# Expert blocks of 127 tokens in place of 128 in the f32r products of a mixture-of-experts stage

## What is computed

```python
def swiglu(h, w_gu, w_down):
    g, u = jnp.split(h @ w_gu, 2, axis=-1)
    return (jax.nn.silu(g) * u) @ w_down

def moe_swiglu(h, w_router, w_gu, w_down):          # 512 tokens, 8 experts, TOP_K = 2
    logits = (xt @ w_router).astype(F32)
    top_logit, top_e = lax.top_k(logits, TOP_K)
    gates = jax.nn.softmax(top_logit, axis=-1)
    ...                                             # sort the 1024 assignments by expert
    y = swiglu(x_of_expert, w_gu[e], w_down[e])     # 1024 -> 2 x 3584 -> 1024
    ...                                             # out[token] += gate * y
```

## Time and profile before

| | us |
|---|---|
| median of 3 runs | 2503.71 |
| lowest and highest run | 2499.23 and 2504.51 |
| profiled execution, its own time | 2502.86 |
| its span, first to last instruction | 2501.2 |
| outside the span | 1.7 |
| expert stage, first to last f32r product of the units | 1273.2 to 2405.6 |

### The profile page before, as it was taken

How to read it: one execution, slowest core, us unless ns; L and a number is a source line. 1 busy time by engine, 2 the same in 40 slices (tenths; PEclk the granted TensorE clock), 3 DMA queues, 4 the chain that set the end, 5 groups by cost and what they waited for, 6 DMA issues and landing times.

```text
span 2501.2 us, 35301 instructions
## 1 busy us (share of the span) xinstructions
PE 2373.3 (95%) x14626; PEld 1811.2 (72%) x14626; DVE 1599.1 (64%) x1807; ACT 1213.6 (49%) x1252; POOL 204.4 (8%) x214
## 2 busy tenths in 40 slices
PE   7999998999999999769979999999999999999977
PEld 4555555588888886768767788777887778777856
DVE  7997776323232334694366688667876688667864
ACT  3645343221222223654245577556765577556753
POOL 4007533000000000000000000001000000000010
PEclk9999998999999999889979999999999999999988
DMA  7668220433332232534177799779987799778960
GB/s 196 195 207 243 84 68 26 148 105 100 101 101 93 101 101 90 175 128 160 43 253 272 280 383 376 276 271 322 394 318 277 270 382 391 257 274 310 394 241 34
DMA packets 259806, 527.94 MB, mean 211 GB/s; under 512 B 19526, under 2 KB 61098, under 8 KB 256986
## 3 DMA queue, kind: packets, MB, share of 16 engines
q1 hardware_dynamic: 230250, 481.30, 54.4%
q0 software_dynamic: 6208, 25.78, 3.4%
q10 hardware_dynamic: 23184, 18.55, 2.3%
HBM read 496.03 MB, written 45.81 MB: 217 GB/s over the span
## 4 chain that ended last, share of the span: by engine, by line
PE 79%; DVE 11%; DMA 3%; ACT 3%; issue 2%; POOL 2%; ACTq 0%; POOLq 0%; DVEq 0%; SPq 0%
PE psum L1898 36%; PE psum L1424 17%; PE psum L1723 6%; PE psum L1961 4%; PE psum L1273 2%; PE psum L1994 2%; PE psum L1299 2%; PE psum L2053 2%; PE psum L1496 1%; PE psum L1938 1%; DVE stages L840 1%; DVE stages L850 1%; DVE stages L845 1%; DVE stages L841 1%; POOL stages L1091 1%
## 5 line engine op out<-in xcount | busy, mean ns | idle before, releaser
L1898 PE MATMUL psum<-stages_r 128*128 128x512 f32 x4032 | 951.7, 394 | 1.2 <-DVE stages_r L3500 0.6
L3500 DVE TENSOR_TENSOR stages_r<-kept,stages_r 128x2048 fp32r<-128x2048 f32 x336 | 769.6, 2291 | 270.3 <-ACT stages_r L2514 269.8
L1898 PEld LDWEIGHTS psum<-stages_r 128*128 128x128 f32 x4032 | 749.3, 188 | 173.8 <-issue 18.1
L2514 ACT ACTIVATE stages_r<-kept 128x2048 fp32r<-128x2048 f32 x336 | 643.7, 1916 | 374.5 <-PE psum L1898 319.5
L1424 PE MATMUL psum<-stages_r 128*128 128x512 f32 x1920 | 437.5, 390 | 3.2 <-ACT stages_r L2080 2.7
L1424 PEld LDWEIGHTS psum<-stages_r 128*128 128x128 f32 x1920 | 360.0, 188 | 79.4 <-ACT stages_r L2080 3.1
L3153 DVE TENSOR_TENSOR stages_r<-kept,stages_r 128x2048 fp32r<-128x2048 f32 x54 | 123.8, 2292 | 338.6 <-ACT stages_r L2372 338.6
L2372 ACT ACTIVATE stages_r<-kept 128x2048 fp32r<-128x2048 f32 x54 | 103.5, 1917 | 325.8 <-PE psum L1424 219.1
L1723 PE MATMUL psum<-stages_r,stages_front_r 128*128 128x512 f32 x672 | 152.6, 389 | 0.8 <-issue 0.8
L1723 PEld LDWEIGHTS psum<-stages_r,stages_front_r 128*128 128x128 f32 x672 | 126.1, 188 | 27.3 <-issue 1.2
L1299 PE MATMUL psum<-stages,kept 128*128 128x512 f32 x256 | 115.5, 598 | 0.0
(11 more groups left out here) (445 smaller groups left out, 2346.8 us busy)
## 6 DMA issues: line engine op xcount, KB each, us to landing
kept<-in_moe_w_gu_dram SPq DMA_DIRECT2D x224, 1024.0 KB, 7.9
kept<-in_moe_w_down_dram SPq DMA_DIRECT2D x112, 1024.0 KB, 8.4
kept<-in_ffn_w_gu_dram SPq DMA_DIRECT2D x28, 1024.0 KB, 5.1
kept<-in_ev_w_in_dram SPq DMA_DIRECT2D x16, 1024.0 KB, 8.0
kept<-in_ffn_w_down_dram SPq DMA_DIRECT2D x14, 1024.0 KB, 5.1
s_output_maps<-s_output_maps_by_state SPq DMA_DIRECT2D x32, 256.0 KB, 4.8
kept<-s_input_maps SPq DMA_DIRECT2D x8, 1024.0 KB, 4.9
kept<-s_output_maps SPq DMA_DIRECT2D x8, 1024.0 KB, 6.7
```

The source lines that it names most:

```text
L1898: m = pe.matmul(out_, a, b, start=start and n == 0, stop=stop and n == len(pairs) - 1, skip_group_check=True)
L2514: act.activation(w_high[n % WSLOTS], unit_tile(n), ACT.Copy).then_inc(s_wh, 1)
L3500: dve.tensor_tensor(w_low[n % WSLOTS], unit_tile(n), w_high[n % WSLOTS], ALU.subtract).then_inc(s_ws, 1)
```

## The change

A constant CAP = P - 1 = 127 is introduced, and it takes the place of P wherever the number of tokens of a block is meant and not the 128 partitions: in the stationary operands of the units' f32r products, in the instructions that make these operands and take the results out, in the store of a block and in the plan's limits. The table y_rows keeps 128 rows for each block, so row 127 of a block is no longer stored; a further fill DMA writes these eight rows (those of the blocks of the eight experts) once before the stage. The narrow leftover products and the products of all other stages stay as they are.

```diff
+        CAP = P - 1
...
-        FILLED = 16 * len(range(NE * P, (EXTRA0 + MAXX) * P, T))
+        FILLED = 16 * (1 + len(range(NE * P, (EXTRA0 + MAXX) * P, T)))
...
+            pool.dma_start(y_rows[0:NE * P, :].rearrange("(b p) n -> b p n", p=P)[:, CAP:P, :],
+                           x[0, 0:NE * (P - CAP), :].rearrange("(b p) n -> b p n", p=P - CAP)).then_inc(s_mys, 16)
...
-                pool.dma_start(y_rows[rank * P:(rank + 1) * P, :], yblk[:, 0, :]).then_inc(s_mys, 16)
+                pool.dma_start(y_rows[rank * P:rank * P + CAP, :], yblk[0:CAP, 0, :]).then_inc(s_mys, 16)
...
-                        m = pe.transpose(psum[:, turn_bank(s_), q * P:(q + 1) * P], shid[s_ % 2][:, q * P:(q + 1) * P], ident)
+                        m = pe.transpose(psum[:, turn_bank(s_), q * P:q * P + CAP], shid[s_ % 2][0:CAP, q * P:(q + 1) * P], ident[0:CAP, 0:CAP])
...
-                            m = products(psum[:, bank, :], ((x_[:, kx, 0:P], wh[:, k, :]), (x_[:, kx, P:2 * P], wh[:, k, :]),
-                                                            (x_[:, kx, 0:P], wl[:, k, :])), kx == 0, kx == 7)
+                            m = products(psum[0:CAP, bank, :], ((x_[:, kx, 0:CAP], wh[:, k, :]), (x_[:, kx, P:P + CAP], wh[:, k, :]),
+                                                               (x_[:, kx, 0:CAP], wl[:, k, :])), kx == 0, kx == 7)
...
-                                m = products(psum[:, 4 + hf, :], ((hd[:, f, 0:P], wh[:, k, at]), (hd[:, f, P:2 * P], wh[:, k, at]),
-                                                                  (hd[:, f, 0:P], wl[:, k, at])),
+                                m = products(psum[0:CAP, 4 + hf, :], ((hd[:, f, 0:CAP], wh[:, k, at]), (hd[:, f, P:P + CAP], wh[:, k, at]),
+                                                                     (hd[:, f, 0:CAP], wl[:, k, at])),
...
-            chain.link(dve.tensor_scalar(nxt, beyond, float(P), None, ALU.is_gt))
+            chain.link(dve.tensor_scalar(nxt, beyond, float(CAP), None, ALU.is_gt))
...
-            chain.link(dve.tensor_scalar(rest, rk, float(P), -float(P), ALU.is_ge, ALU.mult))
-            chain.link(dve.tensor_scalar(past, rk, float(P), None, ALU.is_ge))
+            chain.link(dve.tensor_scalar(rest, rk, float(CAP), -float(CAP), ALU.is_ge, ALU.mult))
+            chain.link(dve.tensor_scalar(past, rk, float(CAP), None, ALU.is_ge))
...
```

More of the change, by code:

```diff
@@ L1214, in _ @@
                         hold(1).then_inc(s_ix, 1)
-                        pool.dma_start(y_rows[bass.ds((u + EXTRA0) * P, P), :], yblk[:, 0, :]).then_inc(s_mys, 16)
+                        pool.dma_start(y_rows[bass.ds((u + EXTRA0) * P, CAP), :], yblk[0:CAP, 0, :]).then_inc(s_mys, 16)
             pool.wait_ge(s_mys, extra_pool * 16 + (FILLED + 16 * STORES[NE - 1]))
@@ L2542, in hidden_high @@
                     act.wait_ge(s_ht, hidden_base(i) + (s_ + 1))
-                    act.activation(hid_s[s_ % 2][:, :, 0:P], psum[:, 6 if wide else 6 + s_ % 2, :].rearrange("p (q t) -> p q t", q=4),
-                                   ACT.Copy).then_inc(s_hdA, 1)
+                    act.activation(hid_s[s_ % 2][:, :, 0:CAP],
+                                   psum[:, 6 if wide else 6 + s_ % 2, :].rearrange("p (q t) -> p q t", q=4)[:, :, 0:CAP], ACT.Copy).then_inc(s_hdA, 1)
                 def leftover_silu(s_):
@@ L2554, in unit_act @@
                     used(i, sgate_at(s_, 1))
-                    act.activation(ssil[s_ % 2], psum[:, s_ % 2, :], ACT.Silu).then_inc(s_sil, 1)
+                    act.activation(ssil[s_ % 2][0:CAP], psum[0:CAP, s_ % 2, :], ACT.Silu).then_inc(s_sil, 1)
                     if wide:
@@ L2576, in unit_act @@
                 y_rows_free(i)
-                act.activation(yblk[:, 0, 0:512], psum[:, 4, :], ACT.Copy).then_inc(s_myA, 1)
+                act.activation(yblk[0:CAP, 0, 0:512], psum[0:CAP, 4, :], ACT.Copy).then_inc(s_myA, 1)
             act.wait_ge(s_lg, TC)
@@ L3433, in _ @@
             for m_ in (2, 3):
-                chain.link(dve.scalar_tensor_tensor(out=nxt, in0=beyond, scalar=float(m_ * P), in1=nxt, op0=ALU.is_gt, op1=ALU.add))
+                chain.link(dve.scalar_tensor_tensor(out=nxt, in0=beyond, scalar=float(m_ * CAP), in1=nxt, op0=ALU.is_gt, op1=ALU.add))
                 chain.settle()
@@ L3448, in _ @@
             chain.link(dve.scalar_tensor_tensor(out=extra, in0=over, scalar=0.0, in1=past, op0=ALU.is_ge, op1=ALU.mult))
-            chain.link(dve.tensor_scalar(rk, over, float(P), None, ALU.is_ge))
+            chain.link(dve.tensor_scalar(rk, over, float(CAP), None, ALU.is_ge))
             chain.settle()
-            chain.link(dve.scalar_tensor_tensor(out=rk, in0=over, scalar=float(2 * P), in1=rk, op0=ALU.is_ge, op1=ALU.add))
+            chain.link(dve.scalar_tensor_tensor(out=rk, in0=over, scalar=float(2 * CAP), in1=rk, op0=ALU.is_ge, op1=ALU.add))
             chain.settle()
             chain.link(dve.tensor_tensor(past, rk, toks_(key), ALU.add))
-            chain.link(dve.scalar_tensor_tensor(out=over, in0=rk, scalar=float(P), in1=toks_(big), op0=ALU.mult, op1=ALU.add))
+            chain.link(dve.scalar_tensor_tensor(out=over, in0=rk, scalar=float(CAP), in1=toks_(big), op0=ALU.mult, op1=ALU.add))
             chain.settle()
@@ L3525, in hidden_low @@
                     dve.wait_ge(s_hdA, hidden_base(i) + (s_ + 1))
-                    dve.tensor_tensor(hid_s[s_ % 2][:, :, P:2 * P],
-                                      psum[:, 6 if wide else 6 + s_ % 2, :].rearrange("p (q t) -> p q t", q=4),
-                                      hid_s[s_ % 2][:, :, 0:P], ALU.subtract).then_inc(s_hdr, 1)
+                    dve.tensor_tensor(hid_s[s_ % 2][:, :, P:P + CAP],
+                                      psum[:, 6 if wide else 6 + s_ % 2, :].rearrange("p (q t) -> p q t", q=4)[:, :, 0:CAP],
+                                      hid_s[s_ % 2][:, :, 0:CAP], ALU.subtract).then_inc(s_hdr, 1)
                     if wide:
@@ L3551, in unit_dve @@
                     dve.wait_ge(s_sil, hidden_base(i) + (s_ + 1))
-                    dve.tensor_tensor(shid[s_ % 2], ssil[s_ % 2], psum[:, 2 if wide else 2 + s_ % 2, :], ALU.mult).then_inc(s_hid, 1)
+                    dve.tensor_tensor(shid[s_ % 2][0:CAP], ssil[s_ % 2][0:CAP], psum[0:CAP, 2 if wide else 2 + s_ % 2, :], ALU.mult).then_inc(s_hid, 1)
                     split(i, sup_at(s_, 1) + WSLOTS)
@@ L3567, in unit_dve @@
                 y_rows_free(i)
-                m = dve.tensor_copy(yblk[:, 0, 512:1024], psum[:, 5, :])
+                m = dve.tensor_copy(yblk[0:CAP, 0, 512:1024], psum[0:CAP, 5, :])
                 if wide:
```

## The result

The changed kernel takes 2520.18 us (median of 4 runs, 2518.74 to 2522.82) against 2502.30 us for the kernel before (median of 4 runs, 2499.23 to 2504.51): a ratio of 1.0077, 95% interval 1.0061 to 1.0093. The forecast was 2465 us. The profiled execution took 2522.82 us, its span is 2521.2 us.

The account below looks back on a forecast made before the run. PE's rate was taken to bound the kernel; removing the f32r surplus would save 22 us in wide and 16 us in small units, -38 us from 2502.86 to 2465 us, with a range of 2457 to 2572.

Parts of the forecast that it names:

- What bounds the kernel: PE, busy 95% of the span, sets the stage; changes in the distance between products come through one to one.
- The distances: Start-to-start times of PE products: f32r 226.9 ns, fp32 429.2 (512 moving columns) and 215.9 (256); f32r pays 11.0 ns extra.
- The step that failed: Units' f32r products: a four-column-at-a-time load stops the moving side, gone at 127; 11.0 ns each, 44.4 us over 4032.
- The bounds of that step: Gain on the units' 4032 products: between 0, if the surplus is a fixed cost, and 44.4 us.
- The sum's range: Whole-kernel time of 2458 to 2481 us around 2465, with the bounds of small units and surplus.
- rival 3: Units' product loads no longer hide beneath the products: 92 ns each, +371 us, 2874 us; chance 0.04.
- something else of either sign: Whole kernel: a partial gain or another new wait, without a size; chance 0.06.
- Rival 1: Units' products: surplus belongs to f32r itself or a load going by columns; nothing changes, 2503 us; chance 0.30.
- Rival 2: Block store's 127 rows land on one DMA engine: +88 us, 2591, or 2569 with wide-unit gain; chance 0.15.
- The Trainium skill's rule on fast loads: PE weight loads: fast, in four 32-column chunks, at 128 weights and non-FP32; by its letter 127 loses it.
- Plan, fill, transposes, elementwise work at nothing: Parts beside the products: plan and elementwise 0, fill at most 0.6 us, transposes at most 0.3 us.
- The small units' DMA limit: Small units: DMA needs 116.4 us, level with PE's 116.5 after the gain; 1.5 us a unit lost waiting for tiles.

Follow-up runs that it names:

- e8: Kernel before with each f32r product of the units cut in two, 256 of the 512 moving columns each; 2547.07 us against 2502.99.
- e7: Kernel before with the units' f32r products taking 96 of 128 stationary columns, from column 0; 2507.93 us against 2502.99.
- e13: Whole changed kernel with the operands of the units' products one column later, columns 1 to 127; ratio 0.9996 to the kernel before, 2498.23 us.
- e9: Kernel before with the units' f32r products taking 127 stationary columns, columns 1 to 127; 2499.20 us against 2495.64.
- e4: Kernel before with the units' f32r products taking 124 stationary columns, from column 0; 2501.28 us against 2499.89.
- e3: Kernel before with the units' f32r products taking 126 stationary columns, from column 0; 2518.38 us against 2499.89.
- e5: Kernel before with the units' f32r products taking 125 stationary columns, from column 0; 2517.77 us against 2502.99.
- e14: Kernel before, all 128 columns, with the turned-token buffers (stationary side of gate and up products) moved by 4 bytes; 2512.03 us against 2498.83.
- e18: Kernel before, all 128 columns, with the turned-token buffers (stationary side of gate and up products) moved by 16 bytes; 2507.32 us against 2501.22.
- e2: Changed kernel with products, hidden-value transposes and elementwise work beside them back at 128; plan, fill, store and copies stay at 127; ratio 0.9998 to before.
- e17: Kernel before with the units' f32r products taking 126 stationary columns, columns 2 to 127; 2498.06 us against 2501.22.

## Why the prediction was wrong, point by point

- *What bounds the kernel.* Right. PE is on the path through all units, and a change of a product's distance came through one to one: 5 to 7 ns in 504 products are 2.5 to 3.5 us a unit, and the windows show 2 to 3, in wide and small units alike.
- *The distances.* The readings were right: 226.9, 429.2 and 215.9 ns, so a surplus of some 32 cycles in f32r that fp32 doesn't have. e8 shows that it belongs to each product and not to the moving columns.
- *The step that failed* is the one from there: that 32 cycles are a quarter of 128 columns, a load four columns at a time that stops the moving side, and that it goes away at 127. One number that fitted a quotient was taken for a mechanism. With 96 columns it should have been 24 cycles, 223.3 ns; measured were 230.0 (e7). The row against it stood in the prediction, the recorded load of 188 ns against 190, and was given too little weight. In place of -11.0 ns a product the change brought up to +6.7 ns, 4.8 ns on average.
- *The bounds of that step.* They ran from 0 to -44.4 us. The sum's range, 2458 to 2481, did not even use the lower bound of 0, which gives 2503. No small loss was priced: on the slower side of the products stood rival 3, with 371 us, and an unpriced 0.06 for something else of either sign. Where the trace holds a single width and a single placement, the cost of another one has no sign, and the term should have had a price above nothing too.
- *Why slower.* The last column of the changed operand ends at byte 508 of a piece of 512. Shown: moving the operand by one column takes all the loss away (e13, e9), ending it at byte 496 does too (e4), taking one or two more columns off so that the end stays off the border keeps it (e3, e5), and moving 128 columns makes them lose (e14). Not shown is why. The two distances differ by 16 cycles, 544 and 560, and either can hold for a whole run with the same operands (the changed kernel at 1498.70 us, e18). That looks as if the start of a product were held to a step of 16 cycles and a badly placed load just missed one; it is an inference, and the distances of the narrower loads (549 to 556 cycles) and the mixture in e18 don't fit it well.
- *Rival 1, nothing changes.* Wrong for this placement, right for e13.
- *Rival 2, the store on one DMA engine.* Refuted: 6.2 us to landing, and e2 at 0.9998. Of the two halves of the Trainium skill's rule (DMA: Bandwidth & Descriptors, Why a DMA increments its semaphore by 16 and not by 1) the exception holds here: a direct copy of 127 rows issued from GpSimd behaves as if it were spread over all engines.
- *Rival 3.* It had the sign right and the size wrong, 371 us for 18: the distance is 233.5 ns and not over 300. With half the moving columns the load of 128 still hides (e8, 120.0 ns).
- *The Trainium skill's rule on fast loads* (TensorE: Matmul & The Clock Gate, Weight-path perf modes — Fast Weight Load (FWL) and DoubleRow) has the number of weights, 128, decide, beside the type. It pointed at a loss, which came, but not by its condition: 127 and 126 columns are as fast as 128 if they end at column 128, and 128 are slower if moved by 4 bytes (e9, e17, e14). The measurement decides.
- *Plan, fill, transposes, elementwise work at nothing.* Right (e2). The number of products stayed 4032, so no extra unit ran.
- *The small units' DMA limit.* Not tested, since PE became slower: a DMA share of 1.02 and 382 GB/s where it was 1.03 and 388.
- *The range* 2457 to 2572 holds 2520 only because it reached out to rival 2, which didn't happen. That is luck: its middle had no case of its own.

## What to carry to other kernels

An f32r product whose stationary columns stop one to three columns short of 128 took 233 and not 227 ns here beside 512 moving columns; leave the gap at the front of the piece and not at its end, or load all 128 columns and ignore one. Fewer stationary columns never made a product faster here, down to 64. And when a surplus in a trace happens to equal a neat fraction, change the quantity it is a fraction of by a lot (96 columns, half the moving side) before forecasting from it.

## What the runs showed of the hardware that I had not expected

- The distance depends on where the stationary operand lies: 124 columns take 226.8 ns from column 0 and 233.5 ns from column 1.
- It has two main values, 226.7 and 233.4 ns, that can hold over runs of 72 products (the changed kernel); with 128 columns moved by 16 bytes both occur in one unit with the same token operands (e18).
- 64, 96 and 112 columns take 229 to 232 ns, more than 128 columns with 226.7.
- An f32r product pays 32 cycles beside its moving columns, whether these are 512 or 256 (226.7 and 120.0 ns), an fp32 one 2.5 ns.
